# Where the gate matmuls, the top-k steps and the sigmoids sit around a sparse attention stage

## The reference: what is computed

```python
h = _rmsnorm(x, norm_mix[l])
proj = h @ w_in[l]
(q_sb, k_sb, v_sb, q_sa, k_sa, v_sa,
 q_ix, k_ix, w_ix, g_sb, g_sa) = _split_cols(proj)
...
o_sb = _stick_breaking(q_sb, k_sb, v_sb)
...
o_sa = _dsa_attention(q_sa, k_sa, v_sa, q_ix, k_ix, w_ix, slopes, top_k)
merged = (jax.nn.sigmoid(g_sb) * (o_sb @ w_branch_sb[l])
          + jax.nn.sigmoid(g_sa) * (o_sa @ w_branch_sa[l]))
x = x + merged @ w_out[l]
h2 = _rmsnorm(x, norm_mlp[l])
x = x + jnp.square(jax.nn.relu(h2 @ w_ff1[l])) @ w_ff2[l]
```

## Time and profile before

| | |
|---|---|
| median of 3 runs | 782.27 us |
| the profiled execution: its time, its span | 782.85 us, 781.1 us |
| TensorE (PE) busy | 756.1 us, 97% |
| VectorE (DVE) busy | 401.8 us, 51% |
| ScalarE (ACT) busy | 304.9 us, 39% |
| GpSimd (POOL) busy | 132.6 us, 17% |
| mean granted TensorE clock | 0.995 |

### The profile page before, as it was taken

How to read it: one execution, slowest core, us unless ns; L and a number is a source line. 1 busy time by engine, 2 the same in 40 slices (tenths; PEclk the granted TensorE clock), 3 DMA queues, 4 the chain that set the end, 5 groups by cost and what they waited for, 6 DMA issues and landing times.

```text
span 781.1 us, 9219 instructions
## 1 busy us (share of the span) xinstructions
PE 756.1 (97%) x3588; PEld 598.4 (77%) x3588; DVE 401.8 (51%) x599; ACT 304.9 (39%) x417; POOL 132.6 (17%) x143
## 2 busy tenths in 40 slices
PE   8999999999997999899999999999999999999998
PEld 4768778777775555588887888888888888888886
DVE  5544786687797856455655532243332333233331
ACT  4324653355564766643233442114311342114310
POOL 3103425000002455003301121002200121002100
PEclk9999999999998999999999999999999999999999
DMA  8407331310011212113181223331333223332011
GB/s 291 149 15 211 113 108 56 113 49 28 27 55 54 55 55 55 54 55 111 51 272 52 67 96 108 108 108 58 104 108 107 97 69 105 105 107 91 16 54 54
DMA packets 47842, 70.11 MB, mean 90 GB/s; under 512 B 2608, under 2 KB 27200, under 8 KB 47808
## 3 DMA queue, kind: packets, MB, share of 16 engines
q1 hardware_dynamic: 47808, 69.65, 27.2%
HBM read 65.19 MB, written 2.10 MB: 86 GB/s over the span
## 4 chain that ended last, share of the span: by engine, by line
PE 87%; DVE 6%; ACT 3%; issue 1%; DMA 1%; POOL 1%; SPq 1%; DVEq 0%; ACTq 0%; POOLq 0%
PE ps L387 13%; PE ps L389 13%; PE ps L388 13%; PE ps L380 13%; PE ps L382 12%; PE ps L381 12%; PE ps L1224 2%; PE ps L1260 2%; PE ps L1301 1%; DVE cut_lo L371 1%; PE ps L1206 1%; PE ps L1291 1%; DMA raw<-in_w_in_dram 1%; PE ps L1236 1%; PE ps L1220 1%
## 5 line engine op out<-in xcount | busy, mean ns | idle before, releaser
L387 PE MATMUL ps<-cut_hi,a_hi 128*128 128x512 f32 x480 | 189.2, 394 | 1.0 <-DVE a_lo L808 1.0
L389 PE MATMUL ps<-cut_hi,a_lo 128*128 128x512 f32 x480 | 187.2, 390 | 0.0
L388 PE MATMUL ps<-cut_lo,a_hi 128*128 128x512 f32 x480 | 187.0, 390 | 0.0
L380 PE MATMUL ps<-b_hi,cut_hi 128*128 128x512 f32 (+1 forms) x336 | 127.6, 380 | 0.5 <-DVE b_lo L808 0.5
L381 PE MATMUL ps<-b_lo,cut_hi 128*128 128x512 f32 (+1 forms) x336 | 127.3, 379 | 0.0
L382 PE MATMUL ps<-b_hi,cut_lo 128*128 128x512 f32 (+1 forms) x336 | 127.3, 379 | 0.0
L371 DVE TENSOR_TENSOR cut_lo<-raw,cut_hi 128x2048 fp32r<-128x2048 f32 (+1 forms) x38 | 78.9, 2079 | 57.3 <-ACT cut_hi L349 57.3
L387 PEld LDWEIGHTS ps<-cut_hi,a_hi 128*128 128x128 f32 x480 | 90.1, 188 | 19.8 <-DVE a_lo L808 1.4
L389 PEld LDWEIGHTS ps<-cut_hi,a_lo 128*128 128x128 f32 x480 | 90.1, 188 | 19.1
L388 PEld LDWEIGHTS ps<-cut_lo,a_hi 128*128 128x128 f32 x480 | 90.2, 188 | 17.5
L364 DVE TENSOR_TENSOR cut_lo<-raw,cut_hi 128x2048 fp32r<-128x2048 f32 x24 | 55.0, 2293 | 83.5 <-ACT cut_hi L358 83.5
(11 more groups left out here) (136 smaller groups left out, 896.1 us busy)
## 6 DMA issues: line engine op xcount, KB each, us to landing
raw<-in_w_ff_dram SPq DMA_DIRECT2D x32, 1024.0 KB, 5.4
raw<-in_w_in_dram SPq DMA_DIRECT2D x18, 1024.0 KB, 5.1
gates<-in_x_dram SPq DMA_DIRECT2D x8, 512.0 KB, 4.8
raw<-in_w_out_dram SPq DMA_DIRECT2D x4, 1024.0 KB, 4.9
raw<-in_w_branch_sb_dram SPq DMA_DIRECT2D x2, 1024.0 KB, 4.8
raw<-in_w_branch_sa_dram SPq DMA_DIRECT2D x4, 512.0 KB, 6.0
out_dram<-gates SPq DMA_DIRECT2D x8, 256.0 KB, 2.0
gates<-sp_hi SPq DMA_DIRECT2D x8, 128.0 KB, 2.3
```

The source lines that it names most:

```text
L380: nc.tensor.matmul(dst, w_hi, rhs_hi, start=start, stop=False)
L387: nc.tensor.matmul(dst, l_hi, w_hi, start=start, stop=False)
L388: nc.tensor.matmul(dst, l_hi, w_lo, start=False, stop=False)
L389: return nc.tensor.matmul(dst, l_lo, w_hi, start=False, stop=stop)
```

## The change

Three things are laid out anew.

- The 64 gate pieces of gates 8 to 15. Before, pairs 0 to 13 held 4 pieces each (2 behind each turn), and gate 15's 8 pieces stood around the last `sa_values`. Now pairs 0, 1, 2 hold 3, 3 and 2, pairs 3 to 15 hold 4 each, and 4 stand behind the last `sa_values`. So a gate is complete at the end of pairs 2, 4, 6 and so on, where it was at the end of pairs 1, 3, 5. ScalarE's `gate_out` moves with it, from n = 5, 9, ... to n = 7, 11, ...
- The top-k steps: `topk(7)` behind pairs c = 0, 1, 2, and none behind c = 3, where it was `topk(5)` behind all four.
- The sigmoids of gates 0 to 5 move into the stick-breaking stage (c = 1 to 3, before the exponentials of the attention weights), those of gates 6 and 7 to n = 3 and 5.

```diff
                 if c:
+                    gate_sigmoid(2 * c - 2)
+                    gate_sigmoid(2 * c - 1)
                     act.wait_ge(av_done, c)
...
-                    if q % 4 == 3 and q < 31:
-                        gate_out(8 + q // 4)
+                    if q % 4 == 1 and q >= 5:
+                        gate_out(7 + q // 4)
                 if n % 8 in (2, 4) and n < 32:
                     act_cut(SL_GATE + 5 + n // 8, n % 8 // 2 - 1, 2)
-                if n % 4 == 1 and n < 32:
-                    gate_sigmoid(n // 4)
+                if n in (3, 5):
+                    gate_sigmoid(6 + n // 4)
                 if n % 4 == 3 and n >= 7:
                     gate_sigmoid(7 + n // 4)
...
                 if c == 3:
                     sa_logits(0)
                     sa_logits(1)
-                topk(5)
+                else:
+                    topk(7)
...
+            turns = [(1, 2), (1, 2), (1, 1)] + 12 * [(2, 2)] + [(2, 2), (4, 0)]
+            piece = itertools.count()
+
+            def gate_pieces(n):
+
+                for _ in range(n):
+                    at = next(piece)
+                    gate(8 + at // KD, at % KD, at % KD + 1)
+
             for pair in range(16):
                 sa_turn(2 * pair)
-                if pair < 14:
-                    gate(8 + pair // 2, 4 * (pair % 2), 4 * (pair % 2) + 2)
+                gate_pieces(turns[pair][0])
                 sa_turn(2 * pair + 1)
                 if pair < 14:
                     sa_scores(pair + 2)
-                    gate(8 + pair // 2, 4 * (pair % 2) + 2, 4 * (pair % 2) + 4)
+                gate_pieces(turns[pair][1])
                 if pair and pair % 2 == 0:
                     sa_values(pair // 2 - 1)
-            gate(15, 0, 4)
             sa_values(7)
-            gate(15, 4, 8)
+            gate_pieces(turns[16][0])
```

More of the change, by code:

```diff
@@ L14 @@
+import itertools
 from contextlib import ExitStack
```

## The result

The changed kernel takes 785.9 us (median of 5 runs, 785.88 to 786.96), the kernel before 781.99 us in the same set of runs. The ratio is 1.0047, with a 95% interval of 1.0036 to 1.0058: slower, by 3.9 us between the medians. The 782.27 us given with the kernel before is the median of three of these five executions of it. The profiled execution took 785.88 us with a span of 784.2 us.

The account below looks back on a forecast made before the run. TensorE, busy 97% of the span, was taken as the bound, waiting for VectorE's weights and ScalarE's `gate_out`. Losses of 17.7 against 14.2 gave +3.5, a turn-by-turn walk +2.9; +3.3 was taken: 785.6 us, range 780.5 to 788.2.

Parts of the forecast that it names:

- Stick-breaking pairs: Two more top-k steps behind c = 0, 1, 2 make the fourth pair's second `sum_later` late, costing 2.1 us.
- First turn: First turn of the sparse stage waits 0.9 us instead of 4.6; the half-clock loss of 2.0 us goes.
- Pairs 0 to 2: Turns 4 and 5 wait for VectorE's half slabs, losing 1.0 and 1.1 us, put at 2.0 together.
- Turns 7 to 9: VectorE's cycle with a top-k step outlasts TensorE's work: 0.7, 0.1 and 0.8 us lost, 1.6 together.
- The three blocks: Half slabs at n = 10, 18, 26 wait for a gate and delay `gate_out` and turns: 3.5 + 3.6 + 2.7 us.
- X: The start of gate 9's last matmul, in pair 4, from which the first block's instants were forecast.
- One sign: Expected in ScalarE's timeline: waits of about 3 us for TensorE before the half slabs of n = 10, 18, 26.
- The gains: Losses before in the sparse stage: 4.6 first turn, 2.0 clock, 2.2 last pairs, 3.5 gate starts, 1.9 small waits.
- 3.5 us of the gate starts: Loss before at eight gate starts, where TensorE waits for ScalarE's `gate_out` at a new gate's first piece.
- Rival (a): VectorE not late with half slabs; turns 4, 5, 12, 13, 20, 21, 28, 29 lose nothing: 778.0 us, chance 0.17.
- Rival (b): No change: 3 of 7.6 us saved at half slabs, or top-k steps fit c = 2 better: 782.3 us, chance 0.20.
- Rival (c): Clock falls at one or two of the blocks, 2.0 us each: 788 to 790 us, chance 0.06.

Follow-up runs that it names:

- e5: Kernel before with topk(8), topk(6), topk(5) and none behind the four stick-breaking pairs, six items left for n = 8 to 13: 777.91 us.
- e6: Changed kernel with a semaphore of its own for ScalarE's first half slab, so VectorE's first half waits for that alone: 781.52 us.
- e9: e8 with its six last top-k items at n = 9, 11, 13, 17, 19, 21 in place of n = 8 to 13: 772.64 us.
- e8: Changed kernel with fitted top-k steps, half-slab semaphore, half slabs at n = 4, 5 (ScalarE) and 6, 7 (VectorE) of each eight: 775.05 us.
- e4: Changed kernel with ScalarE's first half slab of each block at n = 3, 11, 19, 27, behind `gate_out`, in place of n = 2, 10, 18, 26: 784.78 us.
- e1: Kernel before with the change's new top-k layout alone: 779.13 us.
- e7: e5 with gate 15's pieces laid behind turns 28, 30, 31 and the last `sa_values`: 776.19 us.

## Why the prediction was right, point by point

The forecast was 785.6 us, and the reason held at each of its places. That the time came out within 0.3 us is in part luck. The change was forecast at +3.3 us from a median of 782.27 and measured at +3.9 from one of 781.99. For the profiled execution 786.1 was forecast and 785.88 measured, but it had 0.48 us in hand before the changed stages began; within them the shift was 3.6 us, where the sum of the terms said 3.5 and the walk from turn to turn 2.9.

- *Stick-breaking pairs, +2.1.* The second `sum_later` is 2.0 us late. e5, which fits the steps, takes 1.9 off turn 0.
- *First turn, 0.9, clock 1.00.* The trace has 0.93, and 1.00 in every window there.
- *Pairs 0 to 2, 2.0.* Printed 0.76 and 0.87. From starts, turn 4 comes 6.86 us behind turn 0 (6.9 forecast) and turn 5 1.90 behind turn 4 (1.9 forecast), which makes the 2.0. e6 shows the cause for turn 4.
- *Turns 7 to 9, 1.6.* Printed 0.55 and 0.65. e9 moves the steps (on e8's layout) and the waits go.
- *The three blocks, 9.8.* This largest term was right in its instants: `gate_out` at X + 2.22 (2.13 forecast), the piece at X + 2.94 (2.88), the second half slab at X + 4.79 (4.57), turn 12 at X + 8.22 (8.0), with X = 265.33. The printed waits of the three blocks add up to 3.19, 3.25 and 2.37 us, for 3.5, 3.6 and 2.7 forecast. One sign was off: ScalarE's waits before its half slabs were to be about 3 us and are 4.38, 3.73 and 3.93. e4 and e6 separate the term: the waits at gates 10, 12, 14 come from the order on ScalarE, those at turns 12, 20, 28 from VectorE's wait for the second half. What the forecast did not say is that the two overlap, so that they are not 9.8 us to be had one by one: taking the first away (3.8 printed) let turn 12's wait grow by 0.8, and with a fall of the clock gave 1.1 to 2.2 us in the whole.
- *The gains, 14.2 before.* e1 gained 3.2 us of the 3.7 worked out for the first turn, its clock and the delay; e7's tail gained 1.7 of 2.2. The 3.5 us of the gate starts and the 1.9 of small waits were not measured by themselves.

Rival (a), that VectorE would not be late, fell: it was late by the amounts worked out, and e6 shows what its absence gives. Rival (b), no change, fell with the measured interval, which lies wholly above 1. Rival (c) was not the changed kernel's profiled execution, but it exists: two of its five runs took 786.95 us at a mean clock of 0.998, the others 785.9 at 1.0. That is 1.1 us and not the 2.0 of the rival. Where it sits in this kernel no trace shows; in the profiled executions of e4 and e6 such a fall sits at the first block. For the rule of the Trainium skill (TensorE: Matmul & The Clock Gate, A second HAM failure mode: psum-queue depth-cycling), that short idles between matmul groups can drop the clock, these two traces agree (0.70 and 0.63), and the changed kernel's trace, with the same 1.59 us wait and no fewer waits ahead of it at 1.00, does not.

The change as a whole: it shortened a stop of 4.6 us to 0.9, took away about 2.0 us of half clock and hid the gate starts where no half slab stands ahead, but moved four pieces from where VectorE's and ScalarE's half slabs needed their cover, and put a half slab ahead of the `gate_out` that waits for the same matmul.

## What to carry to other kernels

When filler work is moved on one engine, look at every wait on another engine that names its end: of two instructions released by the same event, the one that others wait for belongs first. A gap that is filled in one place was often the cover of another queue's late step, so list what each piece of filler hid before it moves. And a wait that covers two halves of a job where the first is done should name the first.

## What the runs showed of the hardware

The granted clock fell behind waits far shorter than the 4.6 us stop: behind 2.00 us in e4 (turn 12) and behind 1.59 us in e6 (gate 10), each in a stretch with several other short waits ahead, while 1.68 us in the earlier trace rows and 1.59 us in the changed kernel left it at 1.00. So one kernel has executions about 1.1 us apart (785.9 and 786.95, at mean clocks of 1.0 and 0.998), e6 even 1.9 us apart (780.4 and 782.2 in the middle of its two groups, at 1.0 and 0.997), and a difference of 1 us between single executions of such a kernel says nothing. What decides it in one execution stays open here.
